# Two-block transformer on one core: softmax divided behind the values, a product tile kept ahead in the mixer's head, two memory key tiles ahead of a factor

## The reference, cut to what matters

```
mixer:   proj = rms_norm(x) @ w_in             # q_g, k_g, v_g, q_lat, kv_lat
         q_g, k_g normed per head, rotated (rope); c_q, c_kv normed latents
         GQA: 8 query heads, 2 key heads of 64;  MLA: 8 heads of 96, values 64
         p = softmax(q @ k^T * scale) ; o = p @ v        # 512 queries x 512 keys
         x += [rms_norm(o_g), rms_norm(o_m)] @ w_o
memory:  q = rms_norm(x) @ w_mem_q;  k, v = rms_norm(mem) @ w_mem_kv   # 256 tokens
         x += softmax(q @ k^T * scale) @ v @ w_mem_o
```

## Time and profile before

| what | value |
|---|---|
| median of 3 runs | 2342.95 us (2342.58 to 2346.74) |
| profiled execution | 2345.05 us, span 2343.2 us |
| granted TensorE clock, mean | 0.995 |
| PE busy | 2280.9 us, 97% of the span |
| DVE busy | 1360.2 us, 58% |
| ACT busy | 893.6 us, 38% |
| POOL busy | 230.8 us, 10% |
| chain that ended last | PE 86%, DVE 6%, DMA 3%, ACT 2% |

### The profile page before, as it was taken

The page is one execution under the profiler, slowest core; times in us unless marked ns, Lnnn a source line. Parts: engine busy times, 40 slices in busy tenths (PEclk is TensorE's granted clock), DMA queues, the critical chain, the costliest instruction groups (busy, mean ns, idle before and its releaser), DMA issues.

```text
span 2343.2 us, 28475 instructions
## 1 busy us (share of the span) xinstructions
PE 2280.9 (97%) x10844; PEld 1621.2 (69%) x10844; DVE 1360.2 (58%) x2231; ACT 893.6 (38%) x1550; POOL 230.8 (10%) x190
## 2 busy tenths in 40 slices
PE   8999999999999999999999999999999999999998
PEld 6754876344575478744457788888888778888886
DVE  5696654323659755433347757777435665877722
ACT  4485542111437645211133234444223233444421
POOL 2202201000230220100000011000001002000000
PEclk9999999999999999999999999999999999999999
DMA  4300439999530024899973322333333322333331
GB/s 173 99 6 23 140 149 379 410 410 410 218 101 13 19 90 180 333 409 410 410 302 124 86 90 91 99 96 94 99 99 135 112 77 90 99 99 97 101 96 49
DMA packets 112087, 381.63 MB, mean 163 GB/s; under 512 B 16464, under 2 KB 17232, under 8 KB 111696
## 3 DMA queue, kind: packets, MB, share of 16 engines
q1 hardware_dynamic: 108208, 366.80, 44.0%
q0 software_dynamic: 2304, 8.39, 0.9%
q10 hardware_dynamic: 1440, 4.62, 0.5%
HBM read 363.51 MB, written 6.29 MB: 158 GB/s over the span
## 4 chain that ended last, share of the span: by engine, by line
PE 86%; DVE 6%; DMA 3%; ACT 2%; POOL 1%; issue 1%; SPq 0%; POOLq 0%; DVEq 0%; ACTq 0%
PE ps L1346 11%; PE ps L1347 11%; PE ps L1348 11%; PE ps L1643 8%; PE ps L1370 5%; PE ps L1372 5%; PE ps L1371 5%; PE ps L1665 5%; PE ps L1532 3%; PE ps L1391 3%; PE ps L1389 3%; PE ps L1390 3%; PE ps L1482 2%; PE ps L1490 2%; DMA wa<-in_wu 1%; PE ps L1675 1%
## 5 line engine op out<-in xcount | busy, mean ns | idle before, releaser
L2463 DVE TENSOR_TENSOR wlo<-stage,whi 128x1024 fp32r<-128x1024 f32 x262 | 329.4, 1261 | 294.2 <-ACT whi L1782 293.7
L1346 PE MATMUL ps<-hTh,whi 128*128 128x512 f32 x1120 | 442.6, 395 | 0.0
L1348 PE MATMUL ps<-hTh,wlo 128*128 128x512 f32 x1120 | 437.8, 391 | 0.0
L1347 PE MATMUL ps<-hTl,whi 128*128 128x512 f32 x1120 | 437.7, 391 | 0.0
L1782 ACT ACTIVATE whi<-stage 128x1024 fp32r<-128x1024 f32 x262 | 276.0, 1057 | 328.9 <-PE ps L1372 120.6
L1346 PEld LDWEIGHTS ps<-hTh,whi 128*128 128x128 f32 x1120 | 211.2, 189 | 48.2 <-issue 4.7
L1348 PEld LDWEIGHTS ps<-hTh,wlo 128*128 128x128 f32 x1120 | 211.2, 189 | 44.6
L1347 PEld LDWEIGHTS ps<-hTl,whi 128*128 128x128 f32 x1120 | 211.2, 189 | 42.4
L2367 DVE TENSOR_TENSOR ps<-ps,Rs 128x512 f32<-128x512 f32 x124 | 86.1, 699 | 138.9 <-PE ps L1348 124.9
L2370 DVE SCALAR_TENSOR_TENSOR t<-ps,vecs,t 128x511 f32<-128x511 f32 (+1 forms) x176 | 131.1, 745 | 3.7 <-ACT t L1745 0.7
L2367 DVE TENSOR_TENSOR x<-x,ps 128x512 f32<-128x512 f32 x184 | 116.5, 682 | 28.4 <-PE ps L1372 18.0
(11 more groups left out here) (379 smaller groups left out, 4315.9 us busy)
## 6 DMA issues: line engine op xcount, KB each, us to landing
stage<-in_wpk SPq DMA_DIRECT2D x268, 512.0 KB, 3.6
wa<-in_wd SPq DMA_DIRECT2D x56, 512.0 KB, 15.3
wa<-in_wu SPq DMA_DIRECT2D x54, 512.0 KB, 15.1
wa<-in_wg SPq DMA_DIRECT2D x46, 512.0 KB, 15.4
ws<-in_wg SPq DMA_DIRECT2D x26, 512.0 KB, 13.4
ws<-in_wu SPq DMA_DIRECT2D x24, 512.0 KB, 11.9
wr<-in_wg SPq DMA_DIRECT2D x24, 512.0 KB, 15.3
stage<-in_wd SPq DMA_DIRECT2D x22, 512.0 KB, 16.4
```

Of the source, the lines that this page charges most:

```text
L1346: pe.matmul(o, h, ah, start=k == 0, stop=False)
L1347: pe.matmul(o, h, al, start=False, stop=False)
L1348: t = pe.matmul(o, lo, ah, start=False, stop=k == 7)
L2463: ve.tensor_tensor(M.wlo[i % NW][:, :], M.stage[i % NSTAGE][:, :], f(M.whi[i % NW][:, :]), ALU.subtract).then_inc(*S.wlo.mark(("w", i)))
```

## The change

1. `total` and `share` go. The probabilities stay undivided; the row sums go to columns of `st` (16 units deep). Once for each pair, `sums` takes the eight reciprocals and spreads them over a 128x512 tile, `shares` transposes it on PE into a bank of its own, and DVE multiplies the copied values of the pair by that bank. The transposes of a unit wait for its exponential directly, come two units behind the scores instead of three, and the values begin LAG = 4 units behind. Of the transposed tiles DVE copies two in four. For the last pair ACT squares the multiplied `oT` instead of the bank.
2. In the head one or two product tiles are made before they are used: `fm` comes ahead of each tick, and the tick of tile q3 goes.
3. In the memory attention key tiles 2 and 3 both stand between the norm's sums and the transposes of its factor.

```
-LAG = 5
+LAG = 4
-DVE_TURN = 1
+DVE_TURN = (1, 3)
...
             if kt == KT - 1:
-                self.do("att_out", kind, l, p, ub[p])
+                b = self.take()
+                self.do("shares", l, p, b)
+                self.do("att_out", kind, l, p, ub[p], b)
                 self.drop(ub[p])
-                if kind == "mix":
-                    self.att_sums(l, p)
+                self.drop(b)
+                self.att_sums(l, p)
...
-            elif i - 2 < nu:
-                self.do("share", kind, l, i - 2)
+            if i > per and i % per == 1:
+                self.do("sums", l, i // per - 1)
             self.tick()
             for p, kt in plan.get(i, []):
                 values(p, kt)
-            if 0 <= i - 3 < nu:
-                turn_p(i - 3)
+            if 0 <= i - 2 < nu:
+                turn_p(i - 2)
...
         proj("ckv")
+        ready.append(self.fm(s, ns))
         self.tick()
         lat("ck", ("ckv",))
         self.do("krope", l, u, i)
         self.drop(u)
+        ready.append(self.fm(s, ns))
         self.tick()
 
         def head_tile(tile):
             proj(tile)
-            self.tick()
+            if tile != "q3":
+                ready.append(self.fm(s, ns))
+                self.tick()
...
-        i, u = self.fm(s, ns)
+        i, u = ready.pop(0)
         self.do("vT", l, u, i)
...
-        self.scale(ns, lambda: key(2))
-        key(3)
+        def keys():
+            key(2)
+            key(3)
+        self.scale(ns, keys)
```

On PE:

```
-            q.wait_ge(*S.dve.at("share", kind, l, n))
+            q.wait_ge(*S.act.at("exp", kind, l, n))
...
+        elif name == "shares":
+            l, p, u = a
+            o = claim(u)
+            q.wait_ge(*S.dve.at("sums", l, POS["mix"][p]))
+            r = M.tmp[4 + POS["mix"][p] % 2]
+            for m in range(NT):
+                t = pe.transpose(o[:, m * 128:(m + 1) * 128], r[:, m * 128:(m + 1) * 128], M.ident)
+            t.then_inc(*S.pe.mark(("shares", l, p)))
```

On VectorE:

```
+        elif name == "sums":
+            l, i = a
+            q.wait_ge(*S.act.at("exp", "mix", l, 8 * i + 7))
+            if i > 1:
+                q.wait_ge(*S.pe.at("shares", l, SEQ["mix"][i - 2]))
+            c, r = 65 + 16 * (i % 2), M.st[:, 128 + 8 * (i % 2):136 + 8 * (i % 2)]
+            ve.reciprocal(r, M.st[:, c:c + 15:2]).then_inc(*S.dve.mark())
+            after_own()
+            ve.tensor_copy(M.tmp[4 + i % 2][:, :].rearrange("p (m h f) -> p m h f", m=NT, h=2),
+                           r.rearrange("p (h m) -> p m h", h=2).unsqueeze(3).to_broadcast([128, NT, 2, 64])).then_inc(
+                *S.dve.mark(("sums", l, i)))
         elif name == "att_out":
-            kind, l, p, u = a
+            kind, l, p, u, *b = a
+            if kind == "mix":
+                q.wait_ge(*S.act.at("oU", l, p))
+                q.wait_ge(*S.pe.at("shares", l, p))
+                o = M.oT[:, POS["mix"][p], :]
+                tt(o, o, M.ps[b[0][0]][:, :], ALU.mult, ("oT", l, p), ("free",) + b[0])
```

On ScalarE the last pair's square:

```
-            copy(M.osq[OSQ[p]][:, :], M.ps[u[0]][:, :], ("osq", l, p), ("free",) + u,
-                 f=ACT.Square)
+            if p == 7:
+                q.wait_ge(*S.dve.at("oT", l, p))
+                q.wait_ge(*S.pool.at("osq_add", l, OSQ_PAST[p]))
+                copy(M.osq[OSQ[p]][:, :], M.oT[:, POS["mix"][p], :], ("osq", l, p), f=ACT.Square)
```

More of the change, by code:

```diff
@@ L1525, in pe_program @@
                 if kind == "mix":
-                    q.wait_ge(*S.act.at("PT", kind, l, NT * g + 3))
-                    q.wait_ge(*S.dve.at("PT", kind, l, NT * g + DVE_TURN))
+                    q.wait_ge(*S.act.at("PT", kind, l, NT * g + 2))
+                    q.wait_ge(*S.dve.at("PT", kind, l, NT * g + 3))
                 else:
@@ L1864, in act_program @@
             i, r = divmod(n, NHEAD[kind] * NT)
-            c = 64 + 4 * (n % 8)
+            c = 64 + 2 * (n % 16)
+            if n > 15:
+                q.wait_ge(*S.dve.at("sums", l, n // 8 - 2))
             q.wait_ge(*S.dve.at("ng", kind, l, n))
@@ L1877, in act_program @@
             PT = M.PT[kind]
-            if n % 4 == DVE_TURN:
+            if n % 4 in DVE_TURN:
                 continue
@@ L1908, in act_program @@
         elif name == "att_out":
-            kind, l, p, u = a
-            q.wait_ge(*S.pe.at("values", kind, l, p))
+            kind, l, p, u, *_ = a
             if kind == "mem":
+                q.wait_ge(*S.pe.at("values", kind, l, p))
                 q.wait_ge(*S.pe.at("point", "memory", l))
@@ L1917, in act_program @@
                 q.wait_ge(*S.dve.at("heads", l, "q0"))
[L1918 to L1922, removed]
-            copy(M.osq[OSQ[p]][:, :], M.ps[u[0]][:, :], ("osq", l, p), ("free",) + u,
-                 f=ACT.Square)
+            copy(M.oT[:, POS["mix"][p], :], M.ps[u[0]][:, :], ("oU", l, p), ("free",) + u)
+            if p == 7:
+                q.wait_ge(*S.dve.at("oT", l, p))
+                q.wait_ge(*S.pool.at("osq_add", l, OSQ_PAST[p]))
+                copy(M.osq[OSQ[p]][:, :], M.oT[:, POS["mix"][p], :], ("osq", l, p), f=ACT.Square)
         elif name == "orow":
@@ L2163, in pool_program @@
         elif name == "att_out":
-            kind, l, p, u = a
+            kind, l, p, u, *_ = a
             if kind == "mem" or p == 7:
                 continue
-            q.wait_ge(*S.act.at("oT", l, p))
+            q.wait_ge(*S.dve.at("oT", l, p))
             q.wait_ge(*S.dve.at("heads", l, ("q1", "q2")[OSQ[p] // 2]))
@@ L2385, in signed_sines @@
         after_own()
[L2387 to L2396, removed]
     def mshare(l, d):
@@ L2599, in dve_program @@
             kind, l, n, u = a
-            c = 64 + 4 * (n % 8)
-            if n > 1:
-                total(kind, l, n - 2)
+            c = 64 + 2 * (n % 16)
             q.wait_ge(*S.pe.at("scores", kind, l, n))
-            if n > 7:
-                q.wait_ge(*S.dve.at("share", kind, l, n - 8))
+            if n > 15:
+                q.wait_ge(*S.act.at("exp", kind, l, n - 16))
             ve.tensor_reduce(M.st[:, c:c + 1], M.ps[u[0]][:, 0:NKEY[kind]], AX.X, ALU.max, negate=True).then_inc(
                 *S.dve.mark(("ng", kind, l, n)))
-            if n > 1:
-                share(kind, l, n - 2)
         elif name == "turn_p":
             kind, l, n, u = a
-            if n % 4 != DVE_TURN:
+            if n % 4 not in DVE_TURN:
                 continue
@@ L2663, in dve_program @@
                 q.wait_ge(*(S.dve if g else S.pool).at("lo", ("y", l), i - 2))
-            q.wait_ge(*S.act.at("oT", l, i))
+            q.wait_ge(*S.dve.at("oT", l, i))
             keys = [("y", l, g, j)]
```

6 lines of the change are left out of this document (1 added, 5 removed).

## The result

The changed kernel takes 2349.89 us (median of 6 runs, 2347.42 to 2352.57) beside 2344.48 for the kernel before on the same chip (2341.53 to 2346.74): a ratio of 1.0023, with a 95% interval of 1.0013 to 1.0033. The forecast was 2337.5, and the time lies above the range of 2331 to 2348. The forecast was subtracted from 2342.95, the median of three runs, where six give 2344.48; against the kernel before it said 5.4 us less, and 5.4 more came. The profiled execution took 2347.42 us, span 2345.5.

The account below looks back on a forecast made before the run. The prediction took PE, busy 97% of the span, as the bound, with room in the head and front. Its terms summed to −2.7 us per layer, twice −5.4 from 2342.95: 2337.5 us, 8-in-10 range 2331 to 2348.

Parts of the forecast that it names:

- Head up to the last product: First mixer's head: wait and slow product near 46 go, two tiles' steps move behind; last product 5.7 us earlier per layer.
- Behind it: Last product to first score: four rounds left instead of three, 28.9 to 29.1 us instead of 21.9; first score net 1.5 later.
- First units and front: First score to first values: first transposed tile 1.5 us earlier, relieved VectorE gives 2.4, lower clock costs 0.4 per layer.
- Shares: Attention: eight sets of four added share transposes on PE, 3.1 us more per layer.
- Pair boundaries: Attention, first value steps of each pair: shorter waits for the last copy, 1.0 us less per layer.
- Other waits: Attention: waits for POOL's power (1.2), for shares (1.0) and at the output's scaling (1.0) go, 3.2 us less per layer.
- Drain: End of the attention: waits grow from 1.9 to 2.9 us, 1.0 more per layer.
- Memory keys: Memory attention: key tile 3 covers a 0.61 us wait for POOL, 0.6 less per layer.
- rival (B): Attention gives nothing: share transposes' 3.1 us paid, seven pair boundaries each wait 0.4 longer, scaling's wait stays; 2347 us, 22% chance.
- rival (A): Head's chain longer: one more round exposed per layer, first score 7.5 us later instead of 1.5; 2349.5 us, 15% chance.
- a head that alone loses over 2 us: Sign of a wrong forecast: the head by itself loses over 2 us.
- an attention of over 119.6 us from first score to the squares' sum: Sign of a wrong forecast: that stretch of the attention takes longer than the 119.6 us before the change.

Follow-up runs that it names:

- e_h1s: `e_t1` with one product kept ahead in the head, each tile's next step queued ahead of that product: 2336.53 us, ratio 0.9965.
- e_t1: `e_att` with VectorE copying one transposed tile of four (the second) instead of two: 2342.16 us, ratio 0.9991.
- e_att5: `e_att` with LAG = 5 instead of 4, the values' steps one unit later: 2343.85 us, ratio 0.9993.
- e_head: The kernel before with the head's edit alone: 2350.15 us, ratio 1.0027.
- e_h1: `e_t1` with one product kept ahead all the way, the last product too, steps one product later, q3's step kept: 2346.08 us, ratio 1.0008.
- e_att: The kernel before with the attention's and memory keys' edits, the head as before: 2346.66 us, ratio 1.0009.
- e_mix2: Repeat run of `e_att` with VectorE copying tiles 0 and 2 in the first pair's two heads, 1 alone in later heads: 2340.50 us, ratio 0.9977.
- e_h2v: `e_t1` with two products kept ahead in the head, the last product not ahead, last two query tiles in one step: 2343.19 us, ratio 0.9996.

## Why the prediction was wrong

Two steps failed, both in the attention: the 2.4 us that a relieved VectorE was to give in the front, and the gain at the pair boundaries, which was a loss. A third, the joined last round of the head, was too small by about 1 us. Term by term:

- **Head up to the last product** (5.7 earlier): right, 5.8; the wait and the slow product near 46 are gone.
- **Behind it** (first score 28.9 to 29.1 behind, net +1.5): the mechanism was right, four rounds behind the last product with a late cosine product, but 30.3 came, net +2.6. The term that was mis-sized is the joined last round: 1.8 was put for q3 behind q2 where 2.7 came (9.5 against 6.8). The forecast took the late norm of k as the price of the lead; `e_h1s` shows that the lead can be had without it.
- **First units and front** (−1.5 −2.4 +0.4): this step failed. First score to first values gained 1.5. The first transposed tile came 3.4 behind the first score where the clock was full (4.35 in layer 0, with the lower clock that I had put at 0.4; the first values came only 0.15 later for it), near the forecast's 3.3. The 2.4 rested on VectorE falling under PE's 1.27 us per unit. With the low parts of the heads, which the forecast left out, it had 1.3, and in this order its work alternated between 2.0 and 0.7 us. Up to the first values the waits for reciprocals and shares went (3.3), and PE now waits 1.1 for VectorE's copy of a transposed tile.
- **Shares** (3.1): about 3.5. The forecast's own 0.41 a set makes 3.3; it took 0.39. The four transposes take 0.49 start to start (136.62 to 137.11 here), but the set behind them then takes 0.36 (137.11 to 137.47) where it takes 0.41 without them:

```profile
136.62 0.66 PE L1550 MATMUL ps<-c,tmp 128*128 128x128 f32 x4
...
137.11 0.60 PE L1499 MATMUL ps<-c,tmp 128*128 128x128 f32 x4
```

- **Pair boundaries** (−1.0): this failed too, and in its sign. The 32 value steps take 38.5 us start to start, against 37.2 before; 0.3 of that is the last pair's start, which the forecast counted with the drain, so +1.0 came where −1.0 was said. The last two pair starts wait about 2 us each, 1.5 to 1.6 before. The forecast held the copy to be done 2.3 to 2.8 us after the values' end and PE to arrive then; with all of VectorE's queue behind a wait for ScalarE, and with the distance a unit shorter, PE arrived first. Between the first values and the last `e_t1` gives 1.9 back, and `e_att5` 3.0, of which 1.2 is only moved to the front.
- **Other waits** (−3.2): about −2.8, by difference. The waits for POOL's power and the shares are gone. The scaling of the output, of which 1.0 was to go, is no faster; the slow one of the earlier trace rows is as slow, and two that were quick before are slow now. The first two rows are the slow pair again; then the second of the four steps in the changed kernel, and last the same step before:

```profile
206.02 1.58 POOL L2213 TENSOR_TENSOR ygl<-tmp,ygh 128x512 fp32r<-128x512 f32 x1 [1.29 <-ACT ygh L1762]
206.40 1.75 DVE L2388 SCALAR_TENSOR_TENSOR tmp<-oT,vecs,raw 128x512 f32<-128x512 f32 x1
```

```profile
203.84 1.44 DVE L2388 SCALAR_TENSOR_TENSOR tmp<-oT,vecs,raw 128x512 f32<-128x512 f32 x1
```

```profile
204.69 0.74 DVE L2370 SCALAR_TENSOR_TENSOR tmp<-oT,vecs,raw 128x512 f32<-128x512 f32 x1
```

  The trace agrees with the rule cited in the forecast (the Trainium skill, SBUF — State Buffer, "Who interferes with whom"): three of the four steps take 1.43 to 1.75 us, and each starts 0.38 behind a POOL step that reads SBUF. Before it was one of four; the other three met no POOL step and took 0.74 to 0.75. The order counts: of another VectorE operation of the kernel before (`hTl<-x,vecs,hTh`) the twelve that started ahead of POOL's took 0.74 to 0.75 as well.
- **Drain** (+1.0): 0.6. The sum still waits for POOL, 0.72, where over 1 was named and 0.77 had been; the last pair's start adds 0.3, and a gap in the first output products 0.3. The last pair's transposes are counted with the shares.

```profile
228.90 1.05 PE L1563 MATMUL ps<-c,raw 128*128 128x1 f32 x8 [0.72 <-POOL raw L2194]
```

- **Memory keys** (−0.6): right, 0.8. The factor's transposes have no wait in front of them, where the earlier trace rows had 0.61:

```profile
293.19 0.60 PE L1344 MATMUL ps<-c,st 128*128 128x128 f32 x4
```

Per layer the misses are 1.1 behind the last product, 2.0 in the front and 2.4 from there to the memory stage, less 0.2 at the memory keys: 5.3, the whole way from −2.7 to +2.7. The +5.4 us lie between rival (B)'s +4.2 and rival (A)'s +6.6, and neither happened. (B) had the attention's mechanism, but +1.0 came at the boundaries and not its +2.8, and it lacked the front and the head. (A)'s further round did not come: the first score was 2.6 us later than before, where it needed over 4.2. Of the forecast's two signs of being wrong, a head that alone loses over 2 us was met clearly (2.6 in the change, 2.7 and 3.5 in `e_head`), and an attention of over 119.6 us from first score to the squares' sum only just: 119.67, against 119.56 before. The memory keys' edit has no run of its own.

## What to carry to other kernels

Keep work ahead of an engine that waits, but queue the waiting chain's next step ahead of it: beside `e_t1`, one product kept ahead cost 4 us by the ratios where the steps were delayed (`e_h1`) and gave 6 where they were not (`e_h1s`). Where a chain runs at its own pace (here some 6 us a round), look for the first step from which it does (here the norm of q0) and at what that step waits for, and not at how much of the chain is left when another engine is done. When an engine's load is judged, add it up unit by unit together with what else falls on the same units, and give the last operation that a consumer waits for to an engine that has no wait in its queue ahead of it.

## What the hardware showed that was not expected

- The runs of one kernel lie 2 to 9 us apart. In the widest the mean granted clock goes with the time: `e_att` from 2341.99 at 0.995 to 2350.93 at 0.988, `e_mix2` from 2335.05 at 0.993 to 2344.18 at 0.990, with the same instructions. In the profiled run of `e_att` (2348.79, 0.989) the lower level, 1.2 GHz, was granted in seven places ahead of the program's end, among them near 46, in the drain at 230 and at 390, beside waits of PE; near 373 it came where PE had been busy with small matmuls and without a gap. The head of before met the lower clock behind the wait for POOL in both layers of all eight profiled kernels that have this head. Where it lasted 3.4 us the first score came 78.1 to 78.2 behind the first sum, where it lasted 6.8, 79.3 to 79.8. A comparison of 0.2% needs many runs, or the marks in the traces.
- In these runs the lower clock cost time where PE's own work decided: a product at 75 us of `e_h2v` took 7.2 instead of 5.6, and the first score came 1.6 later than in the layer without it. Behind the last product of `e_head` the grant was 0.69 over 11 us and VectorE's norms in that layer did not move by 0.1.
